# The third tile's attention split by keys, three tiles' keys inside layer 0's gather and the fourth's behind it

## The reference

```python
q, k = [nope, rope] per head                        # 8 heads, 128 + 64 wide, from rms-normed latents
s = einsum('bqhd,bkhd->bhqk', qblk, k) * scale      # 128 queries by 512 keys
p = softmax(s, axis=-1)
o = einsum('bhqk,bkhd->bqhd', p, v)
x = x + gate * (o @ w_out)
```

```python
s1, i1 = top_k(s[:, :, 0], 16); s2, i2 = top_k(s[:, :, 1], 16)
sc, pos = top_k(s1[..., :, None] + s2[..., None, :], 16)
act = gelu(einsum('td,thkd->thk', hb, u_tab[idx]))
out = einsum('thk,thkd->td', softmax(sc) * act, v_tab[idx])
```

## Time and profile before

| | us |
|---|---|
| median of three runs | 2574.87 |
| the profiled execution | 2579.73 |
| its span, first to last instruction | 2577.7 |
| layer 0's last sum is done | 1780.96 |
| scores of unit 0 begin | 1812.50 |
| tile 2's `out1` begins / is done | 1858.07 / 1872.05 |
| layer 1's first gather is issued | 1902.96 |

### The profile page before, as it was taken

The page is one execution under the profiler, slowest core; times in us unless marked ns, Lnnn a source line. Parts: engine busy times, 40 slices in busy tenths (PEclk is TensorE's granted clock), DMA queues, the critical chain, the costliest instruction groups (busy, mean ns, idle before and its releaser), DMA issues.

```text
span 2577.7 us, 35146 instructions
## 1 busy us (share of the span) xinstructions
PE 1800.8 (70%) x13092; PEld 848.4 (33%) x13092; DVE 1637.6 (64%) x3826; ACT 958.5 (37%) x2627; POOL 982.4 (38%) x896
## 2 busy tenths in 40 slices
PE   7998979887876785546665566557977765555554
PEld 5877656544541241112211122113543311111110
DVE  1534457858995765677766675654366666666665
ACT  2411147535343332335433353333333433333333
POOL 3013123334443433445445444441024445444442
PEclk9999989999897887788887788778988867787778
DMA  8269769999899999999999999996249999999997
GB/s 311 99 241 334 256 244 378 405 360 391 337 376 415 412 400 397 421 407 418 421 418 421 384 421 419 421 422 263 82 195 419 420 421 421 410 417 421 421 417 292
DMA packets 181898, 936.19 MB, mean 363 GB/s; under 512 B 18128, under 2 KB 35408, under 8 KB 82400
## 3 DMA queue, kind: packets, MB, share of 16 engines
q0 software_dynamic: 114912, 808.16, 76.6%
q1 hardware_dynamic: 66816, 125.79, 13.5%
HBM read 932.74 MB, written 1.15 MB: 362 GB/s over the span
## 4 chain that ended last, share of the span: by engine, by line
DMA 41%; PE 35%; DVE 9%; issue 6%; ACT 5%; POOL 4%; another core or an unknown queue 0%; POOLq 0%; DVEq 0%; SPq 0%; ACTq 0%
DMA arena<-in_experts,expert_cur 37%; PE ps L1965 12%; PE ps L1171 12%; DVE arena L2046 4%; POOL arena L1875 4%; DMA wring<-in_ev_w_in 3%; PE ps L1196 2%; ACT diag L1895 2%; PE ps L1183 2%; PE ps L1718 2%; ACT coef L1891 1%; PE ps L1396 1%; PE ps L1756 1%; PE ps L1377 1%; ACT acts L1890 1%
## 5 line engine op out<-in xcount | busy, mean ns | idle before, releaser
L1965 PE MATMUL ps<-arena,diag 64*64 64x512 f32 x6144 | 1014.1, 789 | 664.2 <-ACT diag L1895 644.2
L1875 POOL DMA_INDIRECT arena<-in_experts,expert_cur x768 | 913.8, 1190 | 1325.5 <-PE ps L1965 999.4
L2046 DVE CUSTOM_DVE_ANT_0 arena<-arena 128x1024 f32<-128x1024 f32 x768 | 942.7, 1228 | 596.5 <-DMA arena<-in_experts,expert_cur 587.4
L1965 PEld LDWEIGHTS ps<-arena,diag 64*64 64x64 f32 x6144 | 245.6, 162 | 1344.8 <-ACT diag L1895 967.9
L1890 ACT ACTIVATE acts<-dots 128x2 f32<-128x2 f32 x384 | 78.2, 204 | 1039.2 <-DVE dots L2046 1038.7
L1895 ACT ACTIVATE diag<-consts,coef 128x128 f32<-128x128 f32 x768 | 266.1, 393 | 12.5
L1891 ACT ACTIVATE coef<-acts,gate_cur 128x1 f32<-128x1 f32 x768 | 184.8, 288 | 12.6
L1171 PE MATMUL ps<-wring 128*128 128x256 f32 (+2 forms) x568 | 148.8, 414 | 17.5 <-DMA wring<-in_ev_w_in 15.0
L1171 PEld LDWEIGHTS ps<-wring 128*128 128x128 f32 x568 | 101.3, 197 | 81.9 <-issue 67.4
L1171 PE MATMUL ps<-arena,wring 128*128 128x256 f32 (+1 forms) x576 | 114.4, 358 | 6.4 <-issue 5.6
L1737 POOL DMA_DIRECT2D mods<-straight x48 | 26.7, 558 | 208.6 <-DVEq L1732 204.5
(11 more groups left out here) (337 smaller groups left out, 1798.3 us busy)
## 6 DMA issues: line engine op xcount, KB each, us to landing
wring<-in_w_mod SPq DMA_DIRECT2D x18, 2048.0 KB, 9.3
wring<-in_ev_w_in SPq DMA_DIRECT2D x14, 1024.0 KB, 27.9
arena<-in_w_mod SPq DMA_DIRECT2D x6, 2048.0 KB, 10.8
wring<-in_ev_w_in SPq DMA_DIRECT2D x6, 2048.0 KB, 10.8
arena<-in_experts,expert_cur POOLq DMA_INDIRECT x768, 11.5
wring<-in_p_w_q SPq DMA_DIRECT2D x5, 2048.0 KB, 25.4
wring<-in_ev_w_out SPq DMA_DIRECT2D x3, 2048.0 KB, 27.5
wring<-in_od_w_out SPq DMA_DIRECT2D x2, 2048.0 KB, 8.0
```

What stands on the lines that cost most here:

```text
L1875: nc.gpsimd.indirect_dma_start(ring[:, k % RING, :], None, table, bass.IndirectOffsetOnAxis(ap=expert_cur[:, par, k:k + 1], axis=0),).then ...
L1965: last = nc.tensor.matmul(ps[rows_of(o), sum_bank(G // PH, i, c), :], diag[rows_of(i), slot, rows_of(i)], ring[rows_of(i), slot, D + 512 * ...
L2046: ins = nc.vector.tensor_tensor_reduce(out=ring[:, slot, 0:D], in0=ring[:, slot, 0:D], in1=place, scale=1.0, scalar=0.0, op0=ALU.mult, op1 ...
```

## The change

Tile 2's attention is taken apart by keys. The keys of tiles 0 to 2 are known before tile 3's sums are done, so its queries and, for each head, the scores over 384 keys, exp against the maximum so far, the transposes and the product with the values (not yet divided) become woven stages (`part_pe/act/dve`) in the heads from 25 on, behind `early(2)` and six empty stages. In `second_block` the fourth tile's 128 keys follow for all eight heads at once: scores `st`, the new maximum, exp, transposes `p3T`, the product `o3`, and the merge with the kept half (`half_o`). `out1` of tile 2 then comes ahead of tile 3's units, and the loop runs over units 8 to 15 alone, with the norm, `q1`, `s1` and the ranking of head 32 at steps 10, 11 and 12 and from 12 on. Layer 1's gather waits for `("out1", 2, 1)` in place of the last unit, and its fourth slot waits for the last unit. The part stages hold fixed banks: scores 0 and 1, transposes 2 and 3, the product 3. Tile 3's query weights are loaded a second time behind the sums; `keys1` is loaded there too, no longer inside the gather.

```diff
+TURN_STEP = HC + 2
+AT_STEP = {TURN_STEP + 1: [("q1", 2, 0)], TURN_STEP + 2: [("s1", 2, 0, p) for p in range(2)]}
+PART_STAGES = 16
+FIXED_BANK = {("sc", u): u % 2 for u in range(HC)} | {("pT", u): 2 + u % 2 for u in range(HC)} | {
+    ("o", p): 3 for p in range(HC // 2)}
+def part_stage(s):
+    scores, outputs, turns = s // 3 if s % 3 == 0 else -1, (s - 6) // 3 if s % 3 == 0 else -1, -1
+    if s % 3 == 1:
+        turns = (s - 4) // 3
+    return [p if 0 <= p < HC // 2 else None for p in (scores, outputs, turns)]
...
+            if G == 4 * PH and k == VALUES_SLOT:
+                pool.wait_ge(product.sem, product.count(("oT", UNITS - 1)))
...
+        def part_pe(pe):
+            yield from blank(BLANK_QUERIES)
+            rope_pe(pe, 2)
+            yield
+            nope_pe(pe, 2, 0)
+            yield
+            nope_pe(pe, 2, 1)
+            turn_rope_pe(pe, 2)
+            yield
+            yield
+            for s in range(PART_STAGES):
+                scores, outputs, turns = part_stage(s)
...
+                if scores is not None:
+                    us = [2 * scores + i for i in range(2)]
+                    banks = [out_bank(pe, ("sc", u))[:, 0:KEYS_EARLY] for u in us]
+                    for i, u in enumerate(us):
+                        nc.tensor.matmul(banks[i], qnT[2][:, u, :], knT[:, u, 0:KEYS_EARLY], start=True, stop=False)
...
+                if outputs is not None:
...
+                        last = accumulate(bank[:, i * P:(i + 1) * P],
+                                          [(part_probT[i][:, k * P:(k + 1) * P], vatt[k][:, u * P:(u + 1) * P])
+                                           for k in range(3)])
+                    product.mark(last, ("o", outputs))
+                if turns is not None:
+                    for i in range(2):
+                        u = 2 * turns + i
+                        taken(pe, ("sc", u))
+                        bank = out_bank(pe, ("pT", u))
+                        for k in range(3):
+                            last = nc.tensor.transpose(bank[:, k * P:(k + 1) * P], part_prob[i][:, k * P:(k + 1) * P],
+                                                       const(IDENT))
+                        product.mark(last, ("pT", u))
+                yield
...
+        def part_act(act):
...
+                if turns is not None:
+                    take_turned(act, copy, turns, 0)
+                if s % 3 == 1 and s // 3 < HC // 2:
+                    for i in range(2):
...
+                        free_bank(nc.scalar.activation(part_prob[i], bank[:, 0:KEYS_EARLY], ACT.Exp, bias=nsmax[:, c],
+                                                       scale=SC, accum_out=ssum[:, c]), ("sc", u))
+                yield
+        def part_dve(dve, head_now):
...
+                if scores is not None:
+                    for u in (2 * scores, 2 * scores + 1):
+                        c = col_of(u)
+                        dve_step(V.tensor_reduce(smax[:, c], in_bank(dve, ("sc", u))[:, 0:KEYS_EARLY], AX, ALU.max))
+                        nmax_ready.mark(V.tensor_scalar(nsmax[:, c], smax[:, c], -SC, None, ALU.mult), u)
+                        yield PART
+                if outputs is not None:
...
+                    free_bank(V.tensor_copy(half_o[:, :, outputs, :], bank), ("o", outputs))
+                if turns is not None:
+                    take_turned(dve, V.tensor_copy, turns, 1)
+                yield
...
-                sp.dma_start(keys1, T["keys1"]).then_inc(bc_landed["keys1",], 16)
...
 second_block, sync:
                 load_late(sp, "ukv_3", w_ukv_3, ktiles(T["ukv"], 0, HC * (NOPE + VD)))
+                load_late(sp, "uq_n3", w_uq_n3, ktiles(T["uq_nope"], 0, HC * NOPE))
+                load_late(sp, "uq_r3", w_uq_r3, ktiles(T["uq_rope"], 0, HC * ROPE))
+                sp.wait_ge(product.sem, product.count(("lkv", 3)))
+                load_late(sp, "out1_0", w_out1[0], ktiles(T["od_w_out"], 0, 512))
                 sp.wait_ge(product.sem, product.count(("lq", 3)))
+                load_late(sp, "out1_1", w_out1[1], ktiles(T["od_w_out"], 512, 1024))
                 load_late(sp, "q1_0", w_q1[0], ktiles(T["p_w_q"][1], 0, 256))
+                sp.wait_ge(product.sem, product.count(("st", 1)))
+                sp.dma_start(keys1, T["keys1"]).then_inc(bc_landed["keys1",], 16)
 scalar, ahead of the units:
+                for par in range(2):
+                    act.wait_ge(merged_max, par + 1)
...
+                        last = A_(new_prob[:, par, i, :], bank[:, i * P:(i + 1) * P], ACT.Exp, bias=all_nmax[:, c], scale=SC,
+                                  accum_out=new_sum[:, c])
...
+                    A_(alpha[:, cols], max_diff[:, cols], ACT.Exp, scale=SC).then_inc(alpha_ready, 1)
 vector:
-            FIRST_RANK = (0, 2, 5, 8, RANK_STEPS)
+            FIRST_RANK = (0, 2, 5, 7, 10, 12, RANK_STEPS, RANK_STEPS)
-                rope_queries(2)
...
+                    step(V.tensor_reduce(new_max[:, c], heads(in_bank(dve, ("st", par))), AX, ALU.max))
+                    step(V.tensor_tensor(all_max[:, c], new_max[:, c], smax[:, c], ALU.max))
...
+                    step(V.tensor_tensor(half_o[:, par], half_o[:, par], over(alpha_rec[:, c]), ALU.mult))
...
+                        last = V.scalar_tensor_tensor(out=half_o[:, par, i, :], in0=bank[:, i, :],
+                                                      scalar=all_rec[:, 4 * par + i:4 * par + i + 1],
+                                                      in1=half_o[:, par, i, :], op0=ALU.mult, op1=ALU.add)
 tensor:
-                rope_pe(2)
-                for g in range(2):
-                    nope_pe(2, g)
-                turn_rope_pe(2)
...
+ st (16 matmuls), values_pe(3, 0..1), p3T(0), p3T(1), nope_pe(3, 0), o3(0), o3(1), nope_pe(3, 1),
+ o3T(0), rope_pe(3), o3T(1), out1(2, 0..1), turn_rope_pe(3)
-                for u in range(UNITS + 3):
+                for u in range(HC, UNITS + 3):
 last_sums, gpsimd:
-                pool.wait_ge(product.sem, product.count(("oT", UNITS - 1)))
+                pool.wait_ge(product.sem, product.count(("out1", 2, 1)))
```

More of the change, by code:

```diff
@@ L498, in build @@
         srec = small[:, 472:488]
+        new_max, all_max, all_nmax, max_diff, alpha, new_sum, all_sum, all_rec, alpha_rec = (
+            small[:, 840 + HC * i:840 + HC * i + HC] for i in range(9))
         sTin = small[:, 488:504]
@@ new lines, in _ @@
+                for par in range(2):
+                    product.mark(last[par], ("st", par))
+                for c in range(2):
+                    values_pe(pe, 3, c)
+                for par in range(2):
+                    taken(pe, ("st", par))
+                    bank = out_bank(pe, ("p3T", par))
+                    for i in range(4):
+                        last = TR(bank[:, i * P:(i + 1) * P], new_prob[:, par, i, :], const(IDENT))
+                    product.mark(last, ("p3T", par))
@@ new lines, in _ @@
+                nope_pe(pe, 3, 0)
+                for c in range(2):
+                    taken(pe, ("v", 3, c))
+                for par in range(2):
+                    taken(pe, ("p3T", par))
+                    bank = out_bank(pe, ("o3", par))
+                    for i in range(4):
+                        h = 2 * i + par
+                        last = M(bank[:, i * P:(i + 1) * P], new_probT[:, par, i, :], vatt[3][:, h * P:(h + 1) * P],
+                                 start=True, stop=True)
+                    product.mark(last, ("o3", par))
@@ new lines, in _ @@
+                nope_pe(pe, 3, 1)
+                for par in range(2):
+                    if par:
+                        rope_pe(pe, 3)
+                    taken(pe, ("o3", par))
+                    bank = out_bank(pe, ("o3T", par))
+                    for i in range(4):
+                        last = TR(bank[:, i * P:(i + 1) * P], half_o[:, par, i, :], const(IDENT))
+                    product.mark(last, ("o3T", par))
+                banks = [out_bank(pe, ("out1", 2, c)) for c in range(2)]
@@ new lines, in _ @@
+                for par in range(2):
+                    taken(pe, ("o3T", par))
+                    for c in range(2):
+                        w = late_weights(pe, f"out1_{c}", w_out1[c], KT)
+                        last = accumulate(banks[c], [(oT[2][:, k, :], w[:, k, :]) for k in range(par, KT, 2)], par == 0,
+                                          par == 1)
+                        if par:
+                            product.mark(last, ("out1", 2, c))
+                turn_rope_pe(pe, 3)
```

301 lines of the change are left out of this document (184 added, 117 removed).

## The result

The changed kernel takes 2557.34 us (median of 5 runs, 2555.74 to 2558.5), and the kernel before took 2581.8 beside it (5 runs, 2573.68 to 2586.41): ratio 0.9915, 95% interval [0.989, 0.994]. That is 0.85% faster, more than the 0.5% that this kernel's measurement can tell from no change. The two profiled executions differ by 2579.73 - 2558.50 = 21.2 us, where the forecast's sum was 15.3.

The account below looks back on a forecast made before the run. The gather is bound by its bytes at 421 GB/s, and the 122.0 us hole between gathers costs its length. Terms -20.1 + 1.5 + 3.0 - 1.2 + 1.5 = -15.3 gave 2559.6 us against 2574.87; range 2554 to 2566.

Parts of the forecast that it names:

- a sign of being wrong: Forecast fails if ranking starts later than +25 us behind `out1`, or the rate in the part stages falls under 400.
- Step 1: Last sum to first scores: tile 2's queries leave this stretch, tile 3's norm then ends it; gain 3.6 us.
- Step 2: First scores to `out1`: PE's list 19.9 plus a 1.2 wait for exps, 21.1 for 45.6 us; gain 24.5.
- Step 3: End of `out1` to POOL's first issue: five units inside the ranking, 38.9 us for 30.9; 8.0 given back.
- Step 4: PE's idle places in the hole: matmuls after them at 1.2 GHz; 0 to 5.1 us lost, 1.5 taken.
- Step 5: Weave in layer 0's gather: PE waits some 7 us for bank 3 in three stages; 3 us lost, bounds 0 and 10.8.
- Step 6: Bytes across the gather's edge: `keys1` leaving gives -1.2 us, `q1_1` partly falling into the gather costs 1.5.
- the ring's slack: Layer 0's weave: ACT's gelu-exp changes make four stages 0.8 us late each, absorbed without cost.
- the rival with 0.02: A drain at table loads where exps stand between gelus: four groups 3.5 late, +5 us, 2564.8; chance 0.02.
- the first: Weave costs layer 0's gather its full 10.8 us, clock 3, `q1_1` 2.5: -5.0, 2570, no change told; chance 0.2.
- The second: All losses in weave, clock and `q1_1` load absorbed: -20.1 - 1.2 = -21.3 us, 2553.6; chance 0.14.
- The slower case: DVE and PE out of step in all seven weave heads, 278 us at 364 GB/s: +16.3, 2591; chance 0.02.

Follow-up runs that it names:

- the longer hole: Changed kernel with 12 more keep-busy matmuls over 512 columns on PE ahead of the fourth tile's scores; 2564.64 us in a single run.
- all four edits: Changed kernel with `o` copied before the maxima, `q1_1` loaded early, `s1` copied first, ranking at once; 2553.29 us (ratio 0.9909), again 2549.95 (0.9882).

## Why the prediction was right, and where its sizes were off

The order of events was as forecast, and the station times nearly so: `out1` done at 1842.05 (near 1844), hole tail 38.92 (38.9), first issue 1880.97 (near 1884). Ranking began 22.0 behind `out1` (23 forecast; later than 25 was to be a sign of being wrong), and over the 80 us of part stages (1637 to 1717) the rate was 410 and, run again, 405 (under 400 was to be the other). By steps, gains with a minus:

- **Step 1, the entry:** -4.2 for -3.6 forecast. The norm's pass took 0.75 (L823), where I had put the 1.23 of the earlier trace rows, but a reciprocal of 0.17 that I had left out stands ahead of it; that made 0.2. The other 0.4 came ahead of the scores, where PE now started 0.45 behind ACT's last copy and before 0.93.
- **Step 2, scores to `out1`:** 19.87 for 21.1, so -25.7 for -24.5. The eight exps of 128 columns took 0.37 each, near the lower end of my 0.31 to 0.69, and PE waited 0.26 for them, not 1.2. `out1` itself took 13.75 for 13.98.
- **Step 3, `out1` to the gather:** +8.0 as forecast, but the 38.92 hold 1.5 that belongs to step 4. In the changed kernel run again the same stretch took 37.4, so my count of DVE's work was 1.5 too long.
- **Step 4, the clock:** +1.5 forecast beside step 3, and 0 or 1.5 measured, in another place. The keep-busy group behind the last sum did fall to 1.2 GHz, as in the earlier trace rows, and was done ahead of the norm. The cost came in the last units: rows 1873.94 and 1875.05 of the chain above, 1.11 and 1.71 long. The kernel run again had in their place:

```profile
1876.08 0.66 PE L2840 MATMUL ps<-consts,arena 128*128 128x128 f32 x4 [1.23 <-DVE arena L2732]
1876.83 1.16 PE L1204 MATMUL ps<-arena 128*128 128x128 f32 x8
```

  Same program, 98.36 for 99.85; the granted clock was 0.50 here (1873.9 to 1876.8) and 1.00 there. Of the eight kernels with this tail three have 99.83 to 99.85 and five 98.3 to 98.4 (the longer hole less its 10.16). Keep-busy matmuls stand at the entry and none between these units, where DVE's work leaves PE idle for up to 1.62 at a time. The Trainium skill (TensorE: Matmul & The Clock Gate, What's actually happening) states of a kernel's start that the number of slow matmuls differs between runs of one kernel; these two runs show the like 1870 us in, 99.85 and 98.36.
- **Step 5, the weave:** +3 forecast; the rate says 2.1 and 3.0. The wait was there (PE stands for bank 3, the sums and POOL behind it), its size was not: 2.97 and 3.02 and 0.23, not three of 7. That it makes the loss is not shown (above). What I had called inside the ring's slack, the table changes, may be a second wait under the first. So the 3 came near by terms that were off: two waits of 3 and something more, not three of 7. Of the drain behind a table load, the rival with 0.02, nothing showed: 1.29 and 1.30 from the start of a load to the next exp.
- **Step 6, the bytes:** `q1_1` +1.5 forecast; 1.2 to 2.1 at the ninth issue, nothing at the last dot product. The 0.7 that the stretch behind the first issue did grow from before to after stays open. `keys1` -1.2 can't be told apart: layer 0's last sum came at +0.16 for +1.8 forecast, but its last group's sums happened to run in 1.99, where before they took 3.60, and tile 2's norm, ahead of all this, came 3.6 later.

Together 6 us less was gained in the forecast (15.3) than in the profiles (21.2). Of these 3.5 are the hole (0.6 of step 1, 1.4 of step 2, 1.5 counted twice in steps 3 and 4), 1.6 layer 0's end, as much as that last group's clock, and 0.8 the time behind the first issue. That 2559.6 still lay only 2.3 above the measured median has a share of luck: I hung it on 2574.87, the median of three runs of a kernel that later ran from 2570.47 to 2592.47 with medians near 2580. Beside the kernel before, the medians differ by 24.5, where 15.3 was forecast.

The rivals: the first wanted 364 GB/s over all of the part stages, which had 410 and 405. The second's sum, -21.3, is the measured one, but by other terms: the rate did lose something, and the hole shrank by 2 more. The slower case would have wanted 389 over the whole weave, and the changed kernel had some 421 outside 40 us. Two of their prices were too low: bytes that take 80 us at 421 GB/s take 80 x 421 / 364 = 92.5 at 364, 12.5 more and not 10.8, and for 278 us it is 43.5 and not 37.6. The forecast takes neither up.

## What to carry to other kernels

A hole between two transfers that run at their full rate is worth its length; take from it what depends only on data that is there early, and price it by the chain of waits, station by station: that held here within 4 us of 100. When two waits lie in one stage, take away both before saying what either costs, and look first at how far kernels with the same stage differ: here by 2.0 us, more than what either edit moved. And when order is changed at the end of a chain, look for what the next resource is held by: the fourth slot's wait took back half or more of what earlier ranking gave.

## What the runs showed of the hardware

- The same or nearly the same idle time of PE was followed by work at 2.4 GHz in one run and at 1.2 GHz in another: 2.63 us in two kernels whose work there is the same (granted clock 1.00 and 0.57), and 1.62 and then 1.23 or 1.16 in two runs of one (1.00 and 0.50), worth 1.5 to 1.7 us each. A kernel's profile fixes such a term for that execution alone.
- The first 1500 us, which none of the edits touches, took 1499.4 to 1515.5 in fourteen profiled executions of kernels with the same work there, with 8.6 us between two of the same kernel. Differences under 10 us need segments, not totals.
- How long POOL waited does not tell what the gather lost: waits of 3.50 and 3.96 us (at 1689.02 and 1695.99 in the changed kernel) came with 386 GB/s over 20 us, 1.7 us lost, waits of 4.93 and 4.94 (at 1672.14 and 1679.59 in the kernel with all four edits) with 391, 1.4 lost, and one wait of 8.15 with 1.3 lost.
